# First attention: modulation products in half chunks on two column groups, sent by SyncE, and the bias of two-tile units added by TensorE

## The chip, the cores and the metric

The kernel runs as one program on one core of a Trainium2 chip. The metric is the device time in microseconds (us), as the median of several executions. A core has TensorE (PE: matmuls, with a weight load of its own ahead of each), VectorE (DVE), ScalarE (ACT), GpSimd (POOL) and SyncE (SP). Here SP only sends transfers. Each engine works off its own instructions in order, and they wait for each other by semaphores.

## The reference, cut to what matters

Two models in a row: a block of two layers (a differential attention with a bias by position, a latent attention, each with a gated FFN and a per-layer embedding), and a second block of two layers whose normed input is scaled and shifted by modulation vectors. All numbers are float32. The change touches the differential attention of the first layer and the modulation of the second block's first layer:

```
sc = einsum('bqhcd,bkhcd->bhcqk', q_blk, k) * scale          # 8 heads, c = 2
sc = where(causal_mask(i, s), sc + bias, NEG_INF)            # bias[h, q, k]
a = softmax(sc, axis=-1)
wts = a[:, :, 0] - lam * a[:, :, 1]
o = einsum('bhqk,bkhv->bqhv', wts, v)
o = rms_norm(o, sub_gain) * (1.0 - lam_init)                 # then @ w_o
...
mod_x = (silu_c @ w_mod[i] + b_mod[i])                       # 1024 -> 3072
mod_c = silu_cc @ w_mod[i] + b_mod[i]
sh_x, sc_x, g_x = split(mod_x, 3)
hx = rms_norm_2(x, norm_g[i]) * (1.0 + sc_x) + sh_x
```

There are 256 tokens, 1024 features, 8 heads of this attention. The modulation vectors depend on `c` and `c_ctx` alone, so they can be computed at any time before the second block.

## The kernel before, in words

Weights stream through the kernel in 295 panels of 512 KB. SP sends each into one of six raw slots (L380), in the order of use; it sends panel p when the low half of panel p - 5 has been split off. ACT makes the high half WH (L1817), DVE the low half WL (L1123), and PE multiplies three times (L413 to L415).

The first attention stands between the projections (`first_unit`) and the output projection `l0_o` (`gemm_unit`, panels 24 to 31). It has 16 units: 8 heads by 2 query tiles. A unit of query tile 0 sees one key tile (128 keys), a unit of query tile 1 sees two (256 keys). The order of the work is written out by hand, as a loop over n in which each engine takes another unit. In round n PE does the two score products of unit n (L724), then five modulation products (`fill(filler)`, L559), the values of a head whose two units are done (L732, written to G), and the transposes of the probabilities of unit n - 2 (`turn`, L633). DVE adds the bias to the scores of unit n (L1351), takes the row maximum (L1204), and scales the probabilities of unit n - 1 (L1179 to L1185). ACT does the exponentials (L1867) and copies the transposed probabilities (L1856) and the values (L1966). POOL squares each head's result (L2479).

After the last unit come the norms of heads 0 to 3 and 4 to 7: the sum over squares on DVE (L1356), the root on ACT (L1976), the reciprocal (L1363) and the products (L1367) on DVE, the transposes on PE (`heads_turn`, L741), and the two halves of the result: XH by ACT (L1982), XL by DVE (L1376). The first unit of `l0_o` starts with heads 0 to 3. On ACT the order is: transposed heads 0 to 3 (L1982), then the root of heads 4 to 7 (L1976).

The modulation vectors of the second block come from products with a stationary tile of 32 columns (`SC[:, k, :]`, silu of `c` and `c_ctx`, the other columns zero) and moving tiles of `w_mod`. The output is 32 partitions of the bank O. The first 2048 of the 3072 columns are made in this attention, as 16 blocks of 128 columns; each block needs 8 products (k = 0 to 7), 128 products in all. They stand as fillers: 12 before the attention, 5 in each of 18 rounds, then 14, 6 and 6 around the transposes of the heads. Block i goes to partitions 32 * (i // 4) and up, so that four blocks in a row go to the same 32 partitions (one column group of TensorE's array). POOL sends the blocks, 512 KB each, into six slots (RN, L2453): two after the first and two after the second step of the bias, the others after `bias_ok`, each when its slot has been used. The remaining 1024 columns and the second layer's come in the FFNs, as `modulate` (L547): four products of 512 columns to four column groups in a row.

Of the kernel before, what the change touches and what calls it, by code (L numbers as in the profile page):

```python
# [32 lines left out]
SPL = 3  # L33
# [3 lines left out]
RMS = 6  # L37
PLAIN = 16
CHUNKS = 8
# [10 lines left out]
START = {}  # L50
# [55 lines left out]
TBLOCKS, TVALS = _b, _v  # L106
# [29 lines left out]
def program(nc, x_tok, wst, wmod, vec, cst, x_t, ctx_t, p_t, pos, pos4, tab, rpb, lam4, grow, y_t):  # L136
    with ExitStack() as ctx:
# [3 lines left out]
        def sem(name):  # L141
            return ctx.enter_context(nc.semaphore(name))
# [25 lines left out]
        SC = sb("SC", [P, KD, 32])  # L168
# [11 lines left out]
        KT0 = mv[:, 2048:4096].rearrange("p (n t) -> p n t", t=T)  # L180
# [14 lines left out]
        TB = B[:, 0:3072].rearrange("p (h k) -> p h k", h=8)  # L195
# [25 lines left out]
        RN = mv[:, 6144:12288].rearrange("p (s c) -> p s c", s=RMS)  # L221
# [61 lines left out]
        def bc(ap, n):  # L283
            return ap.unsqueeze(1).broadcast_to([P, n, ap.shape[1]])
# [38 lines left out]
        m_zero, m_sil, m_used, m_y, m_tr, m_ok = (sem("m_zero"), sem("m_sil"), sem("m_used"), sem("m_y"), sem("m_tr"),  # L323
                                                  sem("m_ok"))
        m_raw = [sem(f"m_raw{i}") for i in range(RMS)]
        sum_step = sem("sum_step")
        r_raw = [sem(f"r_raw{i}") for i in range(2)]
        r_vec = [sem(f"r_vec{i}") for i in range(2)]
# [44 lines left out]
        @block.sync  # L373
        def _(sp):
            sp.dma_start(V[:, :], vec).then_inc(in_vec, 16)

            def panel(p, slot, freed):
                if freed is not None:
                    sp.wait_ge(w_lo, freed)
                sp.dma_start(RAW[:, slot, :], w_ap[p]).then_inc(w_raw[slot], 16)  # L380

            for s in range(RAWS):
                panel(s, s, None)
                if s == 0:
                    sp.dma_start(H[:, 0:4, :], x_t[:, 0:4, :]).then_inc(in_x, 16)
                    sp.dma_start(H[:, 4:8, :], x_t[:, 4:8, :]).then_inc(in_x2, 16)
                if s == 2:
                    sp.dma_start(XTOK, x_tok).then_inc(in_xt, 16)
                if s == 3:
                    sp.dma_start(C[:, :], cst).then_inc(in_cst, 16)  # L390
            turns = NPAN // RAWS
            with sp.Fori(1, turns) as i:
                for s in range(RAWS):
                    panel(i * RAWS + s, s, i * RAWS + s - RAWS + 1)
            for p in range(turns * RAWS, NPAN):
# [9 lines left out]
        def _(pe):  # L405
# [144 lines left out]
            def fill(n):  # L550

                for _ in range(n):
                    i, k = divmod(fills[0], KD)
                    if fills[0] == 0:
                        pe.wait_ge(m_sil, 1)
                    if k == 0:
                        pe.wait_ge(m_raw[i % RMS], 16 * (i // RMS + 1))
                    g, q = i // 4, i % 4
                    m = mm(O[32 * g:32 * g + 32, q * P:(q + 1) * P], SC[:, k, :], RN[:, i % RMS, k * P:(k + 1) * P],  # L559
                           start=(k == 0), stop=(k == KD - 1), skip_group_check=True)  # L560
                    if k == KD - 1:
                        m.then_inc(m_used, 1)
                    fills[0] += 1

            def turn_modulators(dst, made):
# [38 lines left out]
                for _ in range(n):  # L604
                    next(unit, None)

            def attention(s, scores, value, filler=0, behind=None, meanwhile=(0, 0), first=0, last=None, ready=()):
                units = attn_units(s)
                width = 1 if s == "l0" else 2
                for n in range(first, len(units) + 3 if last is None else last):  # L610
                    if behind is not None and n > len(units):
                        advance(behind, meanwhile[n - len(units) - 1])
                    if n < len(units):
                        a = AU0[s] + n
                        if a >= 2:
                            pe.wait_ge(at_ex, 2 * (a - 1))
                        scores(A[2 * (a % 2):2 * (a % 2) + 2], units[n]).then_inc(at_s, 1)
                    if n < len(units) + 2:
                        fill(filler)
                    def turn():  # L620

                        if 2 <= n <= len(units) + 1:
                            nk = units[n - 2][2]
                            a = AU0[s] + n - 2
                            for u, copied in ready:
                                if n - 2 == u:
                                    pe.wait_ge(tm_v, copied)
                            pe.wait_ge(at_p, a + 1)
                            if a >= 1:
                                pe.wait_ge(at_tc, a)  # L630
                            for c in range(width):
                                for k in range(nk):
                                    m = nc.tensor.transpose(ST[c][:, k * P:(k + 1) * P],  # L633
                                                            PRB[a % 3][:, c, k * P:(k + 1) * P], IDT)
                            m.then_inc(at_t, 1)

                    def values():

                        if n >= 3 and units[n - 3][4]:
                            p, qt, nk, job, last = units[n - 3]  # L640
                            pe.wait_ge(at_tc, AU0[s] + n - 2)
                            j = AJ0[s] + job
                            if j >= 2:
# [77 lines left out]
            def scores_l0(out, unit):  # L721
                h, qt, nk, *_ = unit
                for c in range(2):
                    m = mm(out[c][:, 0:nk * P], QT[64 * c:64 * c + 64, h, qt * P:(qt + 1) * P],  # L724
                           KT0[64 * c:64 * c + 64, h, 0:nk * P], start=True, stop=True, skip_group_check=True)
                return m

            def value_l0(out, pt, unit):
# [15 lines left out]

            pe.wait_ge(tm_ev, 8)
            pe.wait_ge(tm_v, 4)
            fill(12)
            pe.wait_ge(bias_ok, 1)
            attention("l0", scores_l0, value_l0, 5)
            fill(14)  # L750
            heads_turn(0)
            fill(6)
            heads_turn(1)
            fill(6)
            for u in range(4):
                gemm_unit(U0["l0_o"] + u, START["l0_o"] + 2 * u, 0, KD, 8, 2,
                          fresh=[XS["l0_o"] - 4] * 4 + [XS["l0_o"]] * 4 if u == 0 else None)
# [114 lines left out]
            for u, (name, g, kt, panels) in enumerate(TOKEN):  # L872
# [22 lines left out]
                if 4 <= u <= 8:  # L895
                    for r in range(2 * u - 8, min(2 * u - 6, 9)):
# [5 lines left out]
            attention("l1", scores_l1, value_l1, 0, first_o, (4, 3), first=2, ready=((1, TVALS),))  # L902
            advance(first_o, 32)
            pe.wait_ge(at_g, AJ0["a"])
            for u in range(1, 4):
# [112 lines left out]
            attention("a", scores_a, value_a, 0, first_o, (2, 2), first=4)  # L1018
            advance(first_o, KD)
            for u in gemm_wide("a_o", 5, None, 1):  # L1020
                pass
# [70 lines left out]
            attention("b", scores_b, value_b, 0, first_o, (6, 3), first=2, ready=((0, TVALS + 10), (1, TVALS + 12)))  # L1092
# [17 lines left out]
        def _(dv):  # L1110
# [236 lines left out]

            def bias_l0(sc, un):
                h, qt, nk, *_ = un
                k0 = 0 if qt == 0 else P  # L1350
                return v.tensor_tensor(sc, sc, bc(TB[:, h, k0:k0 + nk * P], 2), ALU.add)  # L1351

            def heads_summed(g):

# [981 lines left out]
        def _(gp):  # L2336
# [111 lines left out]
            def panels(first, end):  # L2448

                for i in range(first, end):  # L2450
                    if i >= RMS:
                        gp.wait_ge(m_used, i - RMS + 1)
                    gp.dma_start(RN[:, i % RMS, :], wmod[i // 2].rearrange("p (h c) -> (p h) c", h=2)[P * (i % 2):P * (i % 2) + P, :]).then_inc(m_raw[i % RMS], 16)  # L2453

            def gathers(layer, k, i):

# [24 lines left out]
            nextp = 4  # L2481
            for h in range(8):
                upto = min(PLAIN, 6 + (10 * h + 35) // 8)
                panels(nextp, upto)
                nextp = upto
                head_squares(h)
            sum_of_squares("ffn0", H, after("l0_o"))
            ffn(0)
# [203 lines left out]
```

## Time and profile before

| | |
|---|---|
| runs | 1317.41 us median of 3 (1317.01 to 1320.32) |
| the profiled execution | its own time 1318.33 us, span 1316.6 us |
| granted clock of TensorE, mean | 0.997 of full speed |
| busy | PE 1259.6, PE's weight loads 1089.8, DVE 883.2, ACT 689.6, POOL 364.9 us |
| modulation products of the first attention (L559) | 256 records for 128 products, 31.4 us busy, 96.0 to 149.3 us |
| score products (L724) | 64 records for 32 products |
| transfers of `w_mod` by POOL | 16 of 512 KB (this stage), 16 of 1 MB (the FFNs) |

The span is what the profiler saw; the execution's own time has about 1.7 us around it. A float32 product is two records in the trace, so "x10" is five products. Records of PE are longer than the step to the next one, since matmuls overlap; the chain of waits and the starts in a timeline show the step. DVE, ACT and POOL have one record per instruction. In a row of windows the last three numbers are the granted clock of TensorE (1.00 is 2.4 GHz, 0.50 is 1.2 GHz), the busy share of the DMA engines and GB/s; ahead of them stand the stretch, its length and each engine's busy time.

### The profile page before, as it was taken

Reading aid. Unit: us, or ns where it says so; the run is one execution under the profiler, and the core shown is the slowest. Engines: PE = TensorE matmul, PEld = TensorE weight load, DVE = VectorE, ACT = ScalarE, POOL = GpSimd, SP = SyncE. Lnnn points to the kernel's source line nnn. Section 1 sums busy time; section 2 is a strip of 40 time slices with the busy share of each in tenths; the row PEclk is TensorE's granted clock in tenths of the full one; section 3 lists DMA queues with packets and bytes.
Section 4 is the critical chain, followed back from the end, with each engine's and each line's share of the span. In section 5 each row is a group of like instructions: output and inputs, shape, how many; then the busy total and the mean of one; then the engine's idle time right before and its main releaser. Section 6 shows DMA issues by size and latency. Waiting matters only on the chain.

```text
span 1316.6 us, 24170 instructions
## 1 busy us (share of the span) xinstructions
PE 1259.6 (96%) x8884; PEld 1089.8 (83%) x8884; DVE 883.2 (67%) x1388; ACT 689.6 (52%) x1217; POOL 364.9 (28%) x377
## 2 busy tenths in 40 slices
PE   6999999999999999999999999999989999999996
PEld 4887899999998877898999998888755699987666
DVE  6878588666768985558976667753377548453674
ACT  5555455444567777545554447544367515413562
POOL 4942145344321140144444332011012220000022
PEclk9999999999999999999999999999999999999998
DMA  8565247566545532255665664422200364522100
GB/s 311 178 219 193 65 144 263 202 237 237 198 144 175 165 124 96 67 190 173 228 227 208 236 206 135 134 73 95 95 1 1 71 170 144 160 97 80 49 1 33
DMA packets 50361, 191.72 MB, mean 146 GB/s; under 512 B 5792, under 2 KB 6048, under 8 KB 47968
## 3 DMA queue, kind: packets, MB, share of 16 engines
q1 hardware_dynamic: 43488, 158.59, 36.5%
q0 software_dynamic: 6064, 31.33, 6.8%
q8 instruction: 62, 1.02, 0.3%
q10 hardware_dynamic: 720, 0.57, 0.2%
q14 instruction: 27, 0.22, 0.1%
HBM read 189.41 MB, written 1.05 MB: 145 GB/s over the span
## 4 chain that ended last, share of the span: by engine, by line
PE 78%; DVE 9%; ACT 7%; issue 3%; DMA 1%; POOL 1%; SPq 0%; DVEq 0%; ACTq 0%; POOLq 0%
PE G L413 14%; PE G L415 13%; PE G L414 13%; PE A L413 6%; PE A L415 6%; PE A L414 6%; DVE WL L1123 3%; PE R L633 3%; PE R L559 2%; ACT WH L1817 2%; PE A L991 1%; PE R L413 1%; PE R L415 1%; PE R L414 1%; PE G L1000 1%
## 5 line engine op out<-in xcount | busy, mean ns | idle before, releaser
L1123 DVE TENSOR_TENSOR WL<-RAW,WH 128x1024 fp32r<-128x1024 f32 x295 | 382.2, 1302 | 291.8 <-ACT WH L1817 291.4
L1817 ACT ACTIVATE WH<-RAW 128x1024 fp32r<-128x1024 f32 x295 | 310.4, 1057 | 415.1 <-PE G L415 302.7
L413 PE MATMUL G<-XH,WH 128*128 128x256 f32 (+1 forms) x1336 | 400.1, 299 | 9.6 <-DVE WL L1123 6.3
L414 PE MATMUL G<-XL,WH 128*128 128x256 f32 (+1 forms) x1336 | 394.9, 296 | 0.0
L415 PE MATMUL G<-XH,WL 128*128 128x256 f32 (+1 forms) x1336 | 394.9, 296 | 0.0
L413 PEld LDWEIGHTS G<-XH,WH 128*128 128x128 f32 x1336 | 255.3, 191 | 33.2 <-issue 25.8
L414 PEld LDWEIGHTS G<-XL,WH 128*128 128x128 f32 x1336 | 255.5, 191 | 6.3
L415 PEld LDWEIGHTS G<-XH,WL 128*128 128x128 f32 x1336 | 255.5, 191 | 6.3
L413 PE MATMUL A<-HH,WH 128*128 128x256 f32 x352 | 99.8, 283 | 3.7 <-POOL HL L2432 3.7
L414 PE MATMUL A<-HL,WH 128*128 128x256 f32 x352 | 99.6, 283 | 0.0
L415 PE MATMUL A<-HH,WL 128*128 128x256 f32 x352 | 99.5, 283 | 0.0
L2408 POOL CAST XH<-HRS 128x256 fp32r<-128x256 f32 x24 | 11.4, 474 | 267.3 <-DVE HRS L1714 267.3
L1204 DVE TENSOR_REDUCE SM<-A 128x2 f32<-128x1024 f32 (+1 forms) x80 | 67.8, 849 | 17.9 <-PE A L991 12.9
L413 PEld LDWEIGHTS A<-HH,WH 128*128 128x128 f32 x352 | 67.6, 192 | 4.1 <-ACT WH L1817 4.1
L2428 POOL TENSOR_TENSOR HRS<-HSQ,HRS 128x256 f32<-128x256 f32 x22 | 32.0, 1456 | 128.6 <-ACT HRS L2027 128.6
L415 PEld LDWEIGHTS A<-HH,WL 128*128 128x128 f32 x352 | 67.6, 192 | 0.0
L414 PEld LDWEIGHTS A<-HL,WH 128*128 128x128 f32 x352 | 67.6, 192 | 0.0
L1856 ACT ACTIVATE ATT<-R 128x1024 f32<-128x1024 f32 (+3 forms) x56 | 37.7, 674 | 56.9 <-PE R L633 56.9
L413 PE MATMUL G<-WH,XH 128*128 128x512 f32 (+1 forms) x136 | 54.8, 403 | 12.5 <-DVE XL L1149 11.1
L2428 POOL TENSOR_TENSOR HRS<-ATT,HRS 128x256 f32<-128x256 f32 x22 | 32.1, 1457 | 98.1 <-ACT HRS L2027 92.6
L413 PE MATMUL A<-WH,XH 128*128 128x512 f32 x144 | 57.3, 398 | 1.5 <-DVE XL L1444 1.3
L415 PE MATMUL A<-WH,XL 128*128 128x512 f32 x144 | 56.2, 390 | 0.0
(345 smaller groups left out, 2364.7 us busy)
## 6 DMA issues: line engine op xcount, KB each, us to landing
RAW<-in_wst SPq DMA_DIRECT2D x295, 512.0 KB, 3.8
M<-in_wmod POOLq DMA_DIRECT2D x16, 1024.0 KB, 6.6
M<-in_wmod POOLq DMA_DIRECT2D x16, 512.0 KB, 6.3
B<-in_rpb POOLq DMA_DIRECT2D x4, 1024.0 KB, 12.0
H<-in_x_t SPq DMA_DIRECT2D x2, 512.0 KB, 8.3
M<-in_x_tok SPq DMA_DIRECT2D x1, 1024.0 KB, 13.4
M<-in_ctx_t POOLq DMA_DIRECT2D x1, 1024.0 KB, 5.1
out_y<-M SPq DMA_DIRECT2D x2, 384.0 KB, 2.7
```

Source lines behind the costliest of these rows:

```text
L413: mm(out, lh, rh, start=start, stop=False, skip_group_check=True)
L414: mm(out, lh, rl, start=False, stop=False, skip_group_check=True)
L415: return mm(out, ll, rh, start=False, stop=stop, skip_group_check=True)
L559: m = mm(O[32 * g:32 * g + 32, q * P:(q + 1) * P], SC[:, k, :], RN[:, i % RMS, k * P:(k + 1) * P], start=(k == 0), stop=(k == KD - 1), ski ...
L633: m = nc.tensor.transpose(ST[c][:, k * P:(k + 1) * P], PRB[a % 3][:, c, k * P:(k + 1) * P], IDT)
L991: m = mm(out[c][:, 0:nk * P], Q2[64 * c:64 * c + 64, t, qt * P:(qt + 1) * P], K2[64 * c:64 * c + 64, t // 4, k0:512], start=True, stop=Tru ...
L1000: m = mm(out[64 * c:64 * c + 64, 0:T], V2[:, k + (0 if nk == 4 else 2), kv * 64:(kv + 1) * 64], pt[:, c, k, :], start=(k == 0), stop=(k == ...
L1123: v.tensor_tensor(WL[:, slot, :], RAW[:, raw, :], WH[:, slot, :].bitcast(F32), ALU.subtract).then_inc(w_lo, 1)
L1204: v.tensor_reduce(small(80, a, 2), sc, AX, ALU.max, negate=True).then_inc(at_mx, 1)
L1817: act(WH[:, slot, :], RAW[:, raw, :], ACT.Copy).then_inc(w_hi, 1)
L1856: act(att(s, j)[:, 0:width, 0:nk, q * P:(q + 1) * P], RO[:, :].rearrange("p (l k q) -> p l k q", l=2, k=4)[:, 0:width, 0:nk, :], ACT.Copy) ...
L2428: g.tensor_tensor(HID[b], CB[b][:, 0, :], SG[b], ALU.mult).then_inc(f_hid, 1)
```

## The change

1. `w_mod` is laid out otherwise. A chunk is now one k (128 rows) by 1024 of the first 2048 columns. There are still 16 chunks of 512 KB; chunk i has k = i // 2 and half i % 2.
2. `fill` takes a whole chunk: two products of 512 columns with the same stationary tile, to the two column groups 2 * half and 2 * half + 1. There are 32 products instead of 128.
3. They stand in another order: two chunks before the attention, one in each of rounds 1 to 14, none in rounds 0 and 15 to 17, and none around the transposes of the heads.
4. POOL sends chunks 0 to 5 only, the last two after `bias_ok`. SP sends chunks 6 to 15 between panels 32 and 33, each after a wait on the count of used chunks; its loop over panels is cut in two for that.
5. For a unit with two key tiles the bias is added by PE: behind the two score products come two products of the identity with the bias, 256 columns each, into the same banks. DVE adds it only for units with one key tile.

```
-                    i, k = divmod(fills[0], KD)
-                    if k == 0:
-                        pe.wait_ge(m_raw[i % RMS], 16 * (i // RMS + 1))
-                    g, q = i // 4, i % 4
-                    m = mm(O[32 * g:32 * g + 32, q * P:(q + 1) * P], SC[:, k, :], RN[:, i % RMS, k * P:(k + 1) * P],
-                           start=(k == 0), stop=(k == KD - 1), skip_group_check=True)
+                    i = fills[0]
+                    k, half = divmod(i, 2)
+                    pe.wait_ge(m_raw[i] if i < RMS else m_next[i % RMS], 16 * max(1, i // RMS))
+                    for g in range(2):
+                        r = 32 * (2 * half + g)
+                        m = mm(O[r:r + 32, :], SC[:, k, :], RN[:, i % RMS, 512 * g:512 * g + 512],
+                               start=(k == 0), stop=(k == CHUNKS - 1), skip_group_check=True)
+                    m.then_inc(m_used, 1)
...
-                    if n < len(units) + 2:
-                        fill(filler)
+                    if n in filler:
+                        fill(1)
...
                     m = mm(out[c][:, 0:nk * P], QT[64 * c:64 * c + 64, h, qt * P:(qt + 1) * P],
-                           KT0[64 * c:64 * c + 64, h, 0:nk * P], start=True, stop=True, skip_group_check=True)
+                           KT0[64 * c:64 * c + 64, h, 0:nk * P], start=True, stop=qt == 0, skip_group_check=True)
+                if qt:
+                    for c in range(2):
+                        m = mm(out[c][:, 0:nk * P], IDT, TB[:, h, P:P + nk * P], start=False, stop=True, skip_group_check=True)
...
-            fill(12)
+            fill(2)
             pe.wait_ge(bias_ok, 1)
-            attention("l0", scores_l0, value_l0, 5)
-            fill(14)
+            attention("l0", scores_l0, value_l0, range(1, 15))
             heads_turn(0)
-            fill(6)
             heads_turn(1)
-            fill(6)
...
+            held = START["l0_o"] + SPL + RAWS
+            for i in range(RMS, PLAIN):
+                sp.wait_ge(m_used, i - RMS + 1)
+                sp.dma_start(RN[:, i % RMS, :], wmod[i // 2][:, PW * (i % 2):PW * (i % 2) + PW]).then_inc(m_next[i % RMS], 16)
...
-                k0 = 0 if qt == 0 else P
-                return v.tensor_tensor(sc, sc, bc(TB[:, h, k0:k0 + nk * P], 2), ALU.add)
+                return None if qt else v.tensor_tensor(sc, sc, bc(TB[:, h, 0:P], 2), ALU.add)
```

What stands on PE in rounds 3 and 4 of the attention. Before: L724 are the scores, L559 the modulation products, L633 the transposes, L732 the values.

```order
L724 MATMUL A<-M 128x256 x2
L559 MATMUL R<-M,SC 32x128 x5
L633 MATMUL R<-C,RSQ 128x128 x2
L724 MATMUL A<-M 128x128 x2
L559 MATMUL R<-M,SC 32x128 x5
L732 MATMUL G<-M,ATT 128x128 x3
L633 MATMUL R<-C,HSQ 128x128
```

After (L739 scores, L743 bias, L575 modulation, L648 transposes, L750 values):

```order
L739 MATMUL A<-M 128x256 x2
L743 MATMUL A<-B,C 128x256 x2
L575 MATMUL R<-M,SC 32x512 x2
L648 MATMUL R<-C,RSQ 128x128 x2
L739 MATMUL A<-M 128x128 x2
L575 MATMUL R<-M,SC 32x512 x2
L750 MATMUL G<-M,ATT 128x128 x3
L648 MATMUL R<-C,HSQ 128x128
```

Two bias products have come in behind the scores with two tiles, and each five products of 128 columns are two of 512.

The end of the attention on PE, from the last scores to the output projection. Before (L741 are the transposes of the heads, L413 the projection):

```order
L559 MATMUL R<-M,SC 32x128 x5
L633 MATMUL R<-C,ATP 128x128 x2
L732 MATMUL G<-M,ATT 128x128 x3
L559 MATMUL R<-M,SC 32x128 x14
L741 MATMUL A<-C,B 128x128 x8
L559 MATMUL R<-M,SC 32x128 x6
L741 MATMUL A<-C,B 128x128 x8
L559 MATMUL R<-M,SC 32x128 x6
L413 MATMUL G<-XH,WH 128x256
```

After (L759 are the transposes of the heads):

```order
L739 MATMUL A<-M 128x256 x2
L743 MATMUL A<-B,C 128x256 x2
L648 MATMUL R<-C,RSQ 128x128 x2
L750 MATMUL G<-M,ATT 128x128 x3
L648 MATMUL R<-C,HSQ 128x128
L648 MATMUL R<-C,ATP 128x128 x2
L750 MATMUL G<-M,ATT 128x128 x3
L759 MATMUL A<-C,B 128x128 x16
```

No modulation product stands behind the last scores any more, and the transposes of the heads follow each other.

SP's queue around the modulation chunks, after (L381 are panels, L405 chunks of `w_mod`):

```order
L381 DMA RAW<-in_wst 128x1024 x3
L405 DMA M<-in_wmod 128x1024 x10
L381 DMA RAW<-in_wst 128x1024 x3
```

The ten chunks stand between panels 30 to 32 and 33 to 35. In before POOL had them, between its squares of the heads.

## Rows read from the trace of the kernel before

**Rows 1.** The page, busy time of each engine.

```profile
PE 1259.6 (96%) x8884; PEld 1089.8 (83%) x8884; DVE 883.2 (67%) x1388; ACT 689.6 (52%) x1217; POOL 364.9 (28%) x377
```

**Rows 2.** Chain of waits in the attention: start us, us on the chain, what.

```profile
98.82 0.44 PE A L724 x4
...
106.04 0.37 PE R L633 x2
...
106.83 1.21 PE R L559 x10
108.04 0.86 PE G L732 x6
108.91 0.11 PE R L633
109.02 0.63 PE A L724 x4
...
121.28 0.79 PE R L559 x10
```

**Rows 3.** Chain of waits at the attention's end.

```profile
133.35 0.71 DVE A L1351
...
138.51 0.45 PE R L633 x2
...
139.42 0.94 PE G L732 x6
140.36 3.17 PE R L559 x28
...
149.37 0.32 PE G L413
```

**Rows 4.** Timelines of DVE and ACT there: start us, us, what [idle before].

```profile
141.99 1.22 DVE L1356 TENSOR_REDUCE SM<-HRS 128x8 f32<-128x1024 f32 x1 [0.50 <-POOL HRS L2479]
...
147.15 2.72 DVE L1376 SCALAR_TENSOR_TENSOR XL<-A,SM,XH 128x512 fp32r<-128x512 f32 x4
...
144.22 1.26 ACT L1982 ACTIVATE XH<-A,SM 128x512 fp32r<-128x512 f32 x2 [3.44 <-PE A L741]
145.37 0.30 ACT L1976 ACTIVATE SM<-SM 128x8 f32<-128x8 f32 x1
```

**Rows 5.** PE's timeline in the first FFN, four column groups.

```profile
231.55 0.28 PE L415 MATMUL A<-HH,WL 128*128 128x256 f32 x1
231.75 1.06 PE L547 MATMUL R<-M,SV 128*32 128x512 f32 x8
232.75 0.38 PE L413 MATMUL G<-XH,WH 128*128 128x256 f32 x1
```

**Rows 6.** PE's timeline in the second attention, two full-array products, then their successor.

```profile
518.80 1.03 PE L854 MATMUL A<-M 128*128 128x256 f32 x4
519.76 0.70 PE L857 MATMUL A<-B,M 64*128 64x256 f32 x4
```

**Rows 7.** DMA issues from 98 to 99.4 us: KB each, us to landing.

```profile
M<-in_wmod POOLq DMA_DIRECT2D x1, 512.0 KB, 6.1
```

**Rows 8.** PE's timeline at the start, the longest gap of the body, the end; clock of a stretch.

```profile
11.10 0.77 PE L413 MATMUL G<-WH,XH 128*128 128x512 f32 x1 [11.10 <-DVE XL L1149]
...
15.08 0.63 PE L413 MATMUL G<-WH,XH 128*128 128x512 f32 x1
15.51 0.47 PE L414 MATMUL G<-WL,XH 128*128 128x512 f32 x1
...
16.05 0.39 PE L413 MATMUL G<-WH,XH 128*128 128x512 f32 x1
...
375.60 0.36 PE L413 MATMUL A<-HH,WH 128*128 128x256 f32 x1 [1.86 <-POOL HL L2432]
...
1307.04 0.70 PE L468 MATMUL R<-ATP,C 128*128 128x256 f32 x2 [0.59 <-ACT ATP L2327]
...
1309.00:1309.50 0.50, 0.00 (x0) 0.00 (x0) 0.50 (x1) 0.00 (x0) 0.00 (x0) 0.81 0.00 0
```

More of the change, by code:

```diff
@@ L325, in program @@
         m_raw = [sem(f"m_raw{i}") for i in range(RMS)]
+        m_next = [sem(f"m_next{i}") for i in range(RMS)]
         sum_step = sem("sum_step")
@@ L391, in _, with trip @@
             turns = NPAN // RAWS
-            with sp.Fori(1, turns) as i:
+            held = START["l0_o"] + SPL + RAWS
+            def trip(i):
                 for s in range(RAWS):
                     panel(i * RAWS + s, s, i * RAWS + s - RAWS + 1)
+            with sp.Fori(1, held // RAWS) as i:
+                trip(i)
+            for p in range(held // RAWS * RAWS, held):
+                panel(p, p % RAWS, p - RAWS + 1)
+            for i in range(RMS, PLAIN):
+                sp.wait_ge(m_used, i - RMS + 1)
+                sp.dma_start(RN[:, i % RMS, :], wmod[i // 2][:, PW * (i % 2):PW * (i % 2) + PW]).then_inc(m_next[i % RMS], 16)
+            for p in range(held, (held // RAWS + 1) * RAWS):
+                panel(p, p % RAWS, p - RAWS + 1)
+            with sp.Fori(held // RAWS + 1, turns) as i:
+                trip(i)
             for p in range(turns * RAWS, NPAN):
@@ L552, in fill @@
                 for _ in range(n):
-                    i, k = divmod(fills[0], KD)
-                    if fills[0] == 0:
+                    i = fills[0]
+                    k, half = divmod(i, 2)
+                    if i == 0:
                         pe.wait_ge(m_sil, 1)
-                    if k == 0:
-                        pe.wait_ge(m_raw[i % RMS], 16 * (i // RMS + 1))
-                    g, q = i // 4, i % 4
-                    m = mm(O[32 * g:32 * g + 32, q * P:(q + 1) * P], SC[:, k, :], RN[:, i % RMS, k * P:(k + 1) * P],
-                           start=(k == 0), stop=(k == KD - 1), skip_group_check=True)
-                    if k == KD - 1:
-                        m.then_inc(m_used, 1)
+                    pe.wait_ge(m_raw[i] if i < RMS else m_next[i % RMS], 16 * max(1, i // RMS))
[4 more added lines that the diff above has]
+                    m.then_inc(m_used, 1)
                     fills[0] += 1
@@ L605, in advance, with attention @@
                     next(unit, None)
-            def attention(s, scores, value, filler=0, behind=None, meanwhile=(0, 0), first=0, last=None, ready=()):
+            def attention(s, scores, value, filler=(), behind=None, meanwhile=(0, 0), first=0, last=None, ready=()):
                 units = attn_units(s)
@@ L901, in _ @@
                                 + [(1, k) for k in range(8, 16)], T, lambda k: pe.wait_ge(at_g, AJ0["l1"] + k // 2 + 1))
-            attention("l1", scores_l1, value_l1, 0, first_o, (4, 3), first=2, ready=((1, TVALS),))
+            attention("l1", scores_l1, value_l1, (), first_o, (4, 3), first=2, ready=((1, TVALS),))
             advance(first_o, 32)
@@ L1017, in _ @@
             evacuated(pe, U0["a_z"] + 7)
-            attention("a", scores_a, value_a, 0, first_o, (2, 2), first=4)
+            attention("a", scores_a, value_a, (), first_o, (2, 2), first=4)
             advance(first_o, KD)
@@ L1091, in _ @@
             first_o = head_unit("b_o", [(c, k) for c in range(2) for k in range(7)] + [(0, 7), (1, 7)], T, lambda k: pe.wait_ge(at_o, AT_JOBS["a"] + k + 1))
-            attention("b", scores_b, value_b, 0, first_o, (6, 3), first=2, ready=((0, TVALS + 10), (1, TVALS + 12)))
+            attention("b", scores_b, value_b, (), first_o, (6, 3), first=2, ready=((0, TVALS + 10), (1, TVALS + 12)))
             advance(first_o, 2 * KD)
@@ L2452, in panels @@
                         gp.wait_ge(m_used, i - RMS + 1)
-                    gp.dma_start(RN[:, i % RMS, :], wmod[i // 2].rearrange("p (h c) -> (p h) c", h=2)[P * (i % 2):P * (i % 2) + P, :]).then_inc(m_raw[i % RMS], 16)
+                    gp.dma_start(RN[:, i % RMS, :], wmod[i // 2][:, PW * (i % 2):PW * (i % 2) + PW]).then_inc(m_raw[i % RMS], 16)
             def gathers(layer, k, i):
@@ L2479, in head_squares @@
                 g.tensor_tensor(HRS[:, :, (h % 4) * P:(h % 4 + 1) * P], o, o, ALU.mult).then_inc(hn_sq, 1)
-            nextp = 4
+            panels(4, RMS)
             for h in range(8):
-                upto = min(PLAIN, 6 + (10 * h + 35) // 8)
-                panels(nextp, upto)
-                nextp = upto
                 head_squares(h)
@@ L2641 @@
     wmod = np.concatenate([a["w_mod_2"][i] for i in range(2)], 1)
-    near = _tiles(wmod[:, :PLAIN * P]).reshape(PLAIN, PT, P, P).transpose(0, 2, 1, 3).reshape(CHUNKS, P, 2 * PW)
-    far = wmod[:, PLAIN * P:].reshape(KD, P, 2, 2 * PW).transpose(2, 0, 1, 3).reshape(2 * CHUNKS, P, 2 * PW)
-    wmod = np.ascontiguousarray(np.concatenate([near, far]))
+    wmod = np.ascontiguousarray(wmod.reshape(KD, P, 3, 2 * PW).transpose(2, 0, 1, 3)).reshape(3 * KD, P, 2 * PW)
     def twice(x):
```

## The prediction

> **What bounds the kernel now.** I read the page first: TensorE (PE) is busy 96% of the span [rows 1], so a change is worth what it takes from PE's line, or from a wait that PE stands in. Then the chain of waits from 95 to 150 us. The reader is to see that from the first scores at 98.82 us until 133.35 us every piece of the chain is PE's: scores, modulation products (L559), transposes (L633), values (L732), one after the other with no gap [rows 2]. From 133.35 us on VectorE (DVE) and ScalarE (ACT) stand in it [rows 3]. So the stage has two parts with different limits: 34.5 us of PE work end to end, then a tail of latencies. Last I read the timelines of DVE and ACT in the tail for what each step there needs [rows 4].
>
> A check of the first part: up to the last scores, 8 pairs of scores (0.42, the first 0.44, and 0.63), 15 slots of five products (1.21 each, one of them 0.79), turns of 0.37 and 0.11 (one of 0.26), six values of 0.86 [rows 2] make 8.4 + 17.7 + 3.1 + 5.2 = 34.4 us, against 34.5 from 98.82 to 133.35. The model holds, so I replace terms in it.
>
> **The change, part by part.** The sum is made in the profiled execution: span 1316.6 us, its own time 1318.33; the median of the runs is 1317.41, 0.9 lower, and differences are carried over to it.
>
> 1. Modulation products. Gone: 128 products of 128 columns, 0.242 us each (1.21 / 5). New: 16 chunks, each two products of 512 columns for two column groups, F us a chunk. F is not in the trace of before. What is: four such products for four column groups, which take 0.99 us to the next matmul and 1.08 us with the gap before them [rows 5]. Serially, four times 4 x 0.242 would be 3.9, so groups overlap. A second sign: the slot in which the group changes takes 0.79 instead of 1.21 [rows 2]. Below, one product of 512 columns can't take less than four of 128 without their fixed part, about 0.88. So F is 0.88 to 1.08; I take 0.97. Fourteen chunks come before the last scores: 14 x 0.97 = 13.6 instead of 17.7.
>
> The first two chunks go ahead of the attention (0.99 [rows 5] instead of 12 x 0.242), but the attention can't begin before DVE has made the bias, just ahead of the first scores at 98.82 [rows 2]; so that is worth nothing.
>
> 2. Bias of the two-tile units. TensorE adds it with two 128x256 products per unit, B us a unit, 8 units, all on PE's line. Two such full-array products take 0.96 us to their successor in the second attention [rows 6]; without a fixed part twice 0.43. So B is 0.87 to 0.96; I take 0.92: 8 x 0.92 = 7.4 us more. DVE loses eight additions of 0.71, but in the first part DVE isn't on the chain, so only the last is worth something: it stands on the chain at 133.35 us [rows 3].
>
> First part: 13.6 + 7.4 - 17.7 = 3.3 us later at the last scores. With the DVE addition gone: 2.6 us later at the end of the last value (140.36 in before).
>
> 3. The tail. Between the last value and the first matmul of the output projection before has 3.17 us of products (14 of them) [rows 3] and twice six more. All of them go, and the head transposes come as soon as DVE is ready. What is late next is the norm of heads 4 to 7. Its sum (L1356) ends at 143.15 us, 2.8 after the last value, and that doesn't change. In before its square root (L1976) waits until 145.37, because ACT stands in L1982, which waits for transposes that stand behind the 14 products [rows 4]. Now those transposes end at about 1.8 after the value and ACT is free at 2.5. So: root 3.1, reciprocal 3.4, two products of DVE to 4.7, two of the four L1376 (2.72 / 4 each) to 6.1, projection at 6.2 after the value. Before: 149.37 - 140.36 = 9.0. The tail gives 2.8 us.
>
> Sum so far: +2.6 - 2.8 = -0.2 us; with the bounds of F and B from -2.1 to +1.6.
>
> 4. Sending. Ten chunks move from POOL's queue to SP's. There they stand behind panel 32 and ahead of panel 33, whose slot comes free only when the projection (149.37 us [rows 3]) has used a panel; so no weight waits for them. SP waits on the counts of used chunks there, the last (chunk 9) in the middle of the attention. But SP sends chunks 6 and 7 as soon as panel 32 is out and chunks 0 and 1 are used, beside chunks 4 and 5, which POOL still sends at about 99 after the bias. Chunk 4 took 6.1 us to land in before [rows 7], at 105.1; it is needed after the scores of rounds 0 to 3, one turn of 0.26 and chunks 2 and 3, at 98.8 + 2.4 + 2 B + 2 F = 105.0. A wait of 0 to 2.2 us (a third more to land, with two chunks more in the air); I take 0.3, since its issue is the same and only its neighbours change. Moving it off POOL frees 0.5 us a chunk there, which nobody on the chain waits for.
>
> 5. The clock. Cover is gone in the tail: PE's last piece before DVE is done ends 1.9 us after the last scores (turn, value, turn), and the last two transposes of the attention come 4.5 after them (138.51 - 133.29 - 0.71 [rows 3]): empty for 2.6 us. Between the head transposes it is empty from 1.8 to 4.1 us after the value, 2.3 us, and around these gaps stand mostly transposes. In the body of before the longest empty stretch is 1.86 us, with dense work around it, and the clock stays at the full 2.4 GHz [rows 8]. At the end of the kernel the granted clock falls to 1.2 GHz at about 1309.3 us, 1.6 us after the last of a few sparse products [rows 8]. The new tail looks more like the latter. What half speed costs: the first matmuls of the kernel, from 11.10 to 15.5 us, last 0.63 us and start 0.43 apart, the same matmuls from 16.05 on last 0.39 [rows 8], so 4.4 us at the lower level (though the clock's column names it full there), half of it lost: 2.2 us if it all falls on the projection. Bounds: 0 (the clock stays) and 3.5 (the last value and transposes too). I take 2.2.
> The Trainium skill speaks against the change here too: TensorE: Matmul & The Clock Gate (Part 4: PE-mode transpose) says that a transpose doesn't count as a busy TensorE for the clock. By that the tail would be nearly empty from the last scores on; if transposes did count, the fall would be less likely. No row of before settles it.
>
> Total: -0.2 + 0.3 + 2.2 = +2.3 us, 1317.41 + 2.3 = 1319.7.
>
> **The rivals.**
> The clock stays. For it: 1.86 us empty cost nothing twice [rows 8]. Against: the gaps are longer and lie close together. Then the sum is +0.1: 1317.5.
>
> Two groups don't overlap (slower). Place: the 14 slots between scores. If the second product began only with the second half of the first, F would be three halves of 0.43 to 0.45 plus 0.1, or 1.4; wholly serial 1.77 to 1.85. Price: 14 x 0.43 = 6 us to 14 x 0.85 = 12 us: 1325 to 1331. It decides from F = 1.25. For it: scores of 256 columns, two products on two row groups, take 0.63 and not the 0.44 of one [rows 2]. Against: four groups in 0.99 us [rows 5].
> By the Trainium skill (TensorE: Matmul & The Clock Gate, Part 3: Packing small matmuls) matmuls start strictly in program order, and an fp32 product is two records here, so the 1.4 would follow; the same page has three column groups at 2.38 times the speed. The row with four groups fits the second.
>
> Chunks come late (also slower). SP's two early chunks halve what POOL's 4 and 5 get, chunk 4 lands at 107 or later, and chunk 5 too: 2 to 5 us more, 1320 to 1324. Against: SP's land before POOL's first byte, if before's rate there holds.
>
> The products hide beside other matmuls (faster). They use 64 of 128 columns. If the slots of 0.97 shrank by half, 7 us: 1310 to 1312. Against: in before no piece beside a slot got shorter except where the column group changed [rows 2]. That the change doesn't do what it says would show as F = 4 x 0.242 twice, which is the serial case.
>
> **How the numbers follow.** Clock falls: 0.47, 1319.7 (own range 1317.5 to 1321.6). Clock stays: 0.36, 1317.5 (1315.3 to 1319.4). No overlap 0.07; late chunks 0.05; hidden products 0.05. The bound of what can be told from no change is 0.3%, or 4 us: 1313.4 to 1321.4. Faster: the last case, 0.05. Slower: no overlap, half of the late chunks, and the upper end of the falling clock (0.07), 0.17. Same: 0.78. The range goes from the lower end of the staying clock to just above the upper end of the falling clock, 1315.2 to 1321.9; it leaves out the two ends and the rare cases.
>
> **What would show it.** The slots of the modulation products after the scores: 0.97 us each (1.4 or more: no overlap). Bias products: 0.92 us behind each two-tile score. Last scores at about 136.6 us, last value ending at 143, first matmul of the projection at about 149.5. A wait of PE for chunk 4 near 105 us. The granted clock between 138 and 155 us: matmuls of the projection 0.21 us apart at first instead of 0.12 means it fell. From the second unit of the projection on, all must be as before, shifted. The prediction is wrong if the projection starts before 147 or after 152 us, or if the total moves while that start doesn't.

## The result and the profile after

| | before | changed |
|---|---|---|
| time, median of 5 | 1319.06 us (1317.01 to 1320.32) | 1326.05 us (1323.99 to 1329.91) |
| ratio | | 1.0058 (95%: 1.0045 to 1.0071) |
| profiled execution, span | 1316.6 us | 1324.9 us |
| mean granted clock | 0.997 | 0.990 |

The change makes the kernel 7.0 us slower. Forecast were 1319.7 us and a range to 1321.9, from a base of 1317.41 us; the five runs of before here have their median at 1319.06, so 1.65 us of the miss are the base, and the other 4.7 are the difference between +7.0 and the forecast +2.3. Three executions of the case took 1590, 1759 and 3155 us and stay out of all ratios. The page of the changed kernel has TensorE as busy as before [rows 1], over a longer span:

```profile
PE 1260.9 (95%) x8724; PEld 1078.0 (81%) x8724; DVE 876.8 (66%) x1380; ACT 690.0 (52%) x1217; POOL 360.5 (27%) x367
```

Where did the time go? I set the same gaps of TensorE in both traces beside each other. The gap before the first FFN's input is at 178.79 us in before and at 185.44 in the changed kernel, 6.65 later. But the first scores start at 97.35 us instead of 98.77 (both from TensorE's timeline), mostly by chance: the first matmul starts at 9.92 instead of 11.10 [rows 8], and over the eleven variants below that start varies from 9.90 to 11.36. So between the first scores and that gap 8.1 us are lost. Until 382 us nothing more is. There is one more piece, 1.5 us, in a part of the program that the change doesn't touch (below).

The chain of waits in the attention of the changed kernel (start us, us on the chain, what), against [rows 2]:

```profile
98.11 9.90 DMA M<-in_wmod
108.05 1.92 PE R L575 x4
109.97 1.58 PE G L750 x6
...
111.77 1.16 PE A L739 x4
112.92 1.46 PE A L743 x4
114.39 0.98 PE R L575 x4
...
117.14 0.87 PE G L750 x6
118.11 0.63 PE A L739 x4
118.75 1.06 PE A L743 x4
```

There are three things to see. The chain runs over a transfer of `w_mod` issued at 98.11 us: chunk 5. Behind it the same instructions take nearly twice as long (values 1.58 and then 0.87, scores 1.16 and then 0.63, the modulation chunk 1.92 and then 0.98). And in the undisturbed rounds a chunk costs 0.98 us, as forecast, but the bias pair L743 costs 1.06, more than my upper bound of 0.96.

TensorE's timeline in the same kernel (start us, us, what, idle before it and its releaser) shows the waits and the tail:

```profile
97.35 0.93 PE L739 MATMUL A<-M 64*128 64x128 f32 x8 [1.66 <-DVE SM L1361]
...
105.51 1.05 PE L575 MATMUL R<-M,SC 128*32 128x512 f32 x4 [1.83 <-DMA M<-in_wmod]
...
108.05 1.92 PE L575 MATMUL R<-M,SC 128*32 128x512 f32 x4 [0.40 <-DMA M<-in_wmod]
...
140.37 1.13 PE L743 MATMUL A<-B,C 128*128 128x256 f32 x4
141.33 0.38 PE L648 MATMUL R<-C,RSQ 128*128 128x128 f32 x2
...
145.91 0.44 PE L648 MATMUL R<-C,ATP 128*128 128x128 f32 x2 [2.46 <-DVE ATP L1200]
...
152.29 1.97 PE L759 MATMUL A<-C,B 128*128 128x128 f32 x8 [1.99 <-DVE B L1381]
154.30 0.55 PE L428 MATMUL G<-XH,WH 128*128 128x256 f32 x1
154.65 0.42 PE L429 MATMUL G<-XL,WH 128*128 128x256 f32 x1
154.87 0.42 PE L430 MATMUL G<-XH,WL 128*128 128x256 f32 x1
...
158.20 0.28 PE L428 MATMUL G<-XH,WH 128*128 128x256 f32 x1
158.32 0.28 PE L429 MATMUL G<-XL,WH 128*128 128x256 f32 x1
```

Chunk 4 is waited for 1.83 us, chunk 5 another 0.40. In the tail the two gaps of 2.46 and 1.99 us are there. The projection starts at 154.30 with its matmuls 0.22 us apart, and only from 158.20 on they are 0.12 apart. That slow start costs 1.65 us: from the projection's first matmul to the gap at 178.79 and 185.44 it is 29.49 us in before and 31.14 here. The last bias pair (140.37) takes 0.96 us to the transposes behind it, not 1.06; that is taken up again in the section on the prediction. Windows of the same kernel (stretch, its length, TensorE busy, granted clock, DMA share, GB/s) show the clock at these times:

```profile
104.00:106.00 2.00, 0.49 (x4) 1.00 1.02 399
106.00:108.00 2.00, 1.66 (x10) 0.72 1.06 412
110.00:112.00 2.00, 2.00 (x9) 0.50 0.51 145
114.00:116.00 2.00, 2.00 (x12) 1.00 0.00 0
146.00:148.00 2.00, 1.28 (x8) 0.96 0.00 0
148.00:150.00 2.00, 1.67 (x8) 0.50 0.00 0
156.00:158.00 2.00, 2.00 (x11) 0.50 0.04 8
158.00:160.00 2.00, 2.00 (x19) 0.98 0.00 0
```

TensorE was busy for 0.49 of the 2 us from 104 to 106, and then the clock fell to 1.2 GHz, from about 107 to 113.7 us. It fell a second time at 148, until 158. The DMA engines are fully busy at the first fall and idle at the second. The issues from 98 to 99.4 us, which answer to [rows 7]:

```profile
M<-in_wmod POOLq DMA_DIRECT2D x2, 512.0 KB, 8.9
M<-in_wmod SPq DMA_DIRECT2D x1, 512.0 KB, 9.7
```

The 8.9 us are the median of two. Narrower windows of the same view separate them: chunk 4 takes 7.9 us to land (6.1 in before) and chunk 5 9.9. They also show what is in flight beside them. SP issues chunk 6 at 97.1 us, ahead of POOL's chunk 4 (97.6), and it lands in 5.5 us; chunk 7 follows at once and takes 9.7; chunks 8 and 9 go out at 100.3 and 101.8 us, when chunks 2 and 3 have been used. In before chunks 6 and 7 were issued from 100.3 us on, behind 4 and 5 in POOL's queue, and chunks 8 and 9 at 103.6 and 106.3.

The last piece of the time stands at a gap that before has as well [rows 8]:

```profile
382.25 0.36 PE L428 MATMUL A<-HH,WH 128*128 128x256 f32 x1 [1.86 <-POOL HL L2446]
```

and the window behind it, in the columns of the windows above:

```profile
384.00:385.00 1.00, 1.00 (x7) 0.50 0.64 160
```

The same 1.86 us, and this time the clock falls behind it. The next gap (399.46 in before, 407.56 here) is 8.10 us later instead of 6.65, so this fall costs 1.45 us. All 13 profiles of this case have this gap, 1.84 to 1.86 us long; behind it the clock fell in five of them (the changed kernel, e2, e4, e9, e12) and stayed at 1.00 in the other eight, before among them. Nothing here ties it to the change.

### The profile page after: what moved, and what is told of

Read it like the earlier page. It is cut to its first block, busy times and chain, and to the rows that moved or that the text cites. A ratio compares the mean times of both kernels' runs of the same rounds, so it can differ in the third digit from the quotient of the medians.

```text
span 1324.9 us, 23824 instructions
## 1 busy us (share of the span) xinstructions
PE 1260.9 (95%) x8724; PEld 1078.0 (81%) x8724; DVE 876.8 (66%) x1380; ACT 690.0 (52%) x1217; POOL 360.5 (27%) x367
## 4 chain that ended last, share of the span: by engine, by line
PE 79%; DVE 8%; ACT 7%; issue 3%; DMA 1%; POOL 1%; DVEq 0%; SPq 0%; ACTq 0%; POOLq 0%
PE G L428 14%; PE G L429 13%; PE G L430 13%; PE A L428 6%; PE A L430 6%; PE A L429 6%; DVE WL L1138 3%; PE R L648 3%; ACT WH L1831 2%; PE R L428 1%; PE R L430 1%; PE R L429 1%; PE A L1006 1%; PE G L1015 1%; PE R L562 1%
## 5 line engine op out<-in xcount | busy, mean ns | idle before, releaser
L429 PE MATMUL A<-HL,WH 128*128 128x256 f32 x352 | 100.3, 285 | 0.0
```

The lines of the kernel that those rows point to most:

```text
L429: mm(out, lh, rl, start=False, stop=False, skip_group_check=True)
```

## The experiments

All times are medians in us, beside runs of the kernel before on the same chip (1319.15 us beside e1 to e4, 1318.57 beside e5 and e9 to e11, 1318.23 beside e12 to e14). "Stage" is the time from the first scores to the first matmul of the projection in the profiled execution. It is 50.5 us in before and 57.0 in the changed kernel, which then loses 1.65 us more on the projection's slow start.

| run | what | stage | total | ratio to before, 95% |
|---|---|---|---|---|
| e1 | SP sends chunks 4 and 5 first | 51.9 | 1323.78 | 1.0041 (1.0027 to 1.0055) |
| e2 | products of zeros in the waits | 55.0 | 1324.86 | 1.0046 (1.0032 to 1.0059) |
| e3 | products of zeros in the tail | 54.2 | 1323.85 | 1.0034 (1.0024 to 1.0043) |
| e4 | bias by DVE | 50.3 | 1321.03 | 1.0015 (1.0005 to 1.0024) |
| e5 | POOL sends all | 53.2 | 1322.57 | 1.0030 (1.0019 to 1.0040) |
| e9 | e1 and e4 | 48.1 | 1316.55 | 0.9985 (0.9976 to 0.9994) |
| e10 | e9 with zeros around | 47.7 | 1313.96 | 0.9965 (0.9953 to 0.9976) |
| e11 | e9, chunks moved to the tail | 43.1 | 1311.10 | 0.9947 (0.9934 to 0.9960) |
| e12 | before, bias by TensorE alone | 58.6 | 1327.36 | 1.0070 (1.0057 to 1.0083) |
| e13 | e11 with bias by TensorE | 47.7 | 1316.13 | 0.9986 (0.9978 to 0.9995) |
| e14 | e11 with five more zeros | 42.7 | 1311.90 | 0.9958 (0.9944 to 0.9971) |

Single executions of a variant lie 1.5 to 7 us apart, those of before about 3. So terms of 1 to 3 us are read from the traces, and the medians only confirm their sum.

**e1: who comes first on the DMA engines.**

```
+            sp.wait_ge(bias_ok, 1)
+            for i in range(4, RMS):
+                sp.dma_start(RN[:, i % RMS, :], wmod[i // 2][...]).then_inc(m_raw[i], 16)
             for i in range(RMS, PLAIN):      # SP
...
-            panels(4, RMS)                   # POOL
```

> The changed kernel, but SP sends chunks 4 and 5 too, ahead of 6 to 15, after a wait on the bias; POOL sends none of the last twelve. Theory (chunks 4 and 5 land late because SP's 6 to 9 take their share of the DMA engines from another queue): chunk 4 lands in 4 to 6 us, PE waits 0 to 0.3 us for it instead of 2.2, the clock stays at 1.00 in the attention, first scores to first projection matmul 52.0 us instead of 57.0, total about 4.9 us below the changed kernel (1321). Rival (all transfers together are too many, whoever sends them): the wait stays near 2 us, total 1326.

Its stage is 51.9 us, 5.0 less than in the changed kernel. TensorE's timeline has the products of chunks 4 and 5 with no wait:

```profile
104.59 1.13 PE L746 MATMUL A<-B,C 128*128 128x256 f32 x4
105.65 1.05 PE L578 MATMUL R<-M,SC 128*32 128x512 f32 x4
...
107.42 1.05 PE L578 MATMUL R<-M,SC 128*32 128x512 f32 x4
```

and its windows show the granted clock at 1.00 from 98 to 138 us, though the DMA engines are as full as before:

```profile
98.00:106.00 8.00, 6.61 (x35) 1.00 0.88 277
106.00:114.00 8.00, 8.00 (x44) 1.00 0.98 384
```

So it isn't the amount of transfers but their order that costs the wait. The run changes the queue of chunks 4 and 5 together with their place; e5, with all chunks in POOL's queue, has no wait either. Which of SP's chunks 6 to 9 took most of the share no run separates. The profiled span is 5.2 us below the changed kernel's, the median only 2.3. In this profile the clock fell at 22.9 us too, at a gap of 2.77 us in the first projection (1.60 us in the changed kernel's profile, with the clock at 1.00), and the attention began 2 us later. The fall in the tail is still there.

**e2: is the slow stretch the clock's?**

```
+                    if i in (4, 5):
+                        idle(8 if i == 4 else 2)
                     pe.wait_ge(m_raw[i] ...)
+            def idle(n):
+                for _ in range(n):
+                    mm(O[0:30, 0:P], SC[:, 0, 2:32], IDT, start=False, stop=True, skip_group_check=True)
```

> The changed kernel with ten products of zeros (128 columns, added to O) in the two waits for chunks 4 and 5. Theory (the wait of 2.2 us costs 2.7 us more because the clock falls after it): the waits stay, the clock stays at 1.00 from 98 to 140 us, stage 57.0 - 2.7 = 54.3 us, total 1323.3. Rival (the slow stretch at 108 to 114 us has another cause, such as the DMA traffic): still slow, total 1326.

The stage is 55.0 us, 2.0 less, and the clock stays at 1.00 from 104 to 144 us. But in this execution it fell earlier: from about 97 to 100.7 us it was at 0.50, after the gap of 1.67 us before the first scores. That makes TensorE ask later: it is ready for chunk 4 at 105.19 us, and the chunk, issued at 97.7, lands 8.5 us later, at 106.2. So about 1.0 us of waiting is left in place of 1.83, and the zeros cover it, until 106.74. The run agrees with the theory and doesn't isolate it, since the wait shrank as well. What it adds is that the gap that the change opens ahead of the attention (12 products became two chunks) can cost as well; I had put that edit at nothing.

**e3: the tail.**

```
+                    if s == "l0" and n == 17:
+                        idle(9)
                     def turn():
...
+            idle(1)
             heads_turn(0)
+            idle(7)
             heads_turn(1)
```

> The changed kernel with products of zeros in the gaps behind the last scores: nine in the last round before the transposes, one before and seven between the transposes of the heads. Theory (the clock falls in the tail because PE is empty): the clock stays at 1.00 to the projection, whose matmuls start 0.12 us apart at once; 1.9 us less there and about 1.0 less on transposes, total 1323.2. Rival (transposes alone let the clock fall, or the fillers delay the transposes): first projection matmuls still 0.21 us apart, total 1326 or above.

The projection starts at full pace, 0.12 us between its second and third product in TensorE's timeline:

```profile
151.83 0.35 PE L428 MATMUL G<-XH,WH 128*128 128x256 f32 x1 [0.76 <-DVE XL L1399]
152.03 0.28 PE L429 MATMUL G<-XL,WH 128*128 128x256 f32 x1
152.15 0.28 PE L430 MATMUL G<-XH,WL 128*128 128x256 f32 x1
```

and the windows of this run have full clock in the whole tail:

```profile
97.00:104.00 7.00, 6.39 (x22) 0.51 0.87 269
...
144.00:154.00 10.00, 7.80 (x58) 1.00 0.01 2
```

From the start of the last value to the projection it takes 7.15 us instead of 7.48, and the 1.65 us of slow start are gone: 2.0 us for the clock of the tail, close to the 2.2 of the forecast. The fall ahead of the attention came here too (0.51 from 97 to 104 us).

**e4: the bias back on DVE.**

```
-                if qt:
-                    for c in range(2):
-                        m = mm(out[c][:, 0:nk * P], IDT, TB[:, h, P:P + nk * P], ...)
+                return v.tensor_tensor(sc, sc, bc(TB[:, h, k0:k0 + nk * P], 2), ALU.add)
```

> The changed kernel with the bias of all units added by DVE again, as in before; the rest stays. Theory (TensorE's bias costs 8 x 1.06 us on its line and gives back 0.7): pairs of rounds take 4.4 us instead of 5.42, unless DVE is the bound, at 4.1 to 4.5; five free pairs and the first two: 6 us less, but chunk 4 is asked for 2 us earlier and waited for longer, so about 1322. Rival (DVE would have been the bound without TensorE's help): pairs of 5 us or more, total 1325 to 1327.

Stage 50.3 us, 6.7 less. The timeline of TensorE, one wait and one pair of rounds:

```profile
107.55 1.28 PE L575 MATMUL R<-M,SC 128*32 128x512 f32 x4 [4.03 <-DMA M<-in_wmod]
...
117.18 0.70 PE L739 MATMUL A<-M 64*128 64x256 f32 x4
117.81 1.05 PE L575 MATMUL R<-M,SC 128*32 128x512 f32 x4
...
121.54 0.70 PE L739 MATMUL A<-M 64*128 64x256 f32 x4
```

A pair is 121.54 - 117.18 = 4.36 us against 5.42 in the changed kernel and 4.81 in before, with no gap: DVE keeps up, and the rival falls. Part of the gain is eaten by the chunk, asked for sooner and waited for 4.03 us.

**e5: POOL sends all chunks again.** SP's ten sends are gone; POOL sends up to chunk 9 before its first head and two more per head.

> The changed kernel, but POOL sends all chunks in order, as in before (up to chunk 9 before its first head, two more per head). Only the sender is undone. Theory (chunks 6 to 9 in SP's queue take the share of 4 and 5): POOL's own queue keeps the order, chunk 4 lands as in before or sooner (6 us or less), wait for it 0 to 0.8 us instead of 1.83 and 0.40; the clock in the attention stays; stage 52 to 53 us, total 1321 to 1322. Rival (a software queue mixes its own chunks as much): wait about 2 us, total 1326.

There is no wait for a chunk, and chunk 4 lands in 6.6 us. The ratio to before is 1.0030 instead of 1.0058. But the clock was at 0.50 from 100 to 103 us in this execution, so that TensorE asked later. At full clock it would ask 6.3 us after the first scores, at 105.0, and the chunk landed at about 105.5: a wait of half a us, by this estimate. No run shows it.

**e9: both costs out.** e1 and e4 together.

> The changed kernel with two parts altered: SP sends chunks 4 and 5 first, and DVE adds all biases. Theory (late chunks and the bias on TensorE are the two costs beside the clock): no wait for chunks, pairs of 4.36 us as in the run with the bias on DVE, last scores about 30.3 us after the first, then 7.0 + 7.5 us; stage about 45.5 us against 50.5 in before, less 2 us of clock in the tail: total 1319.1 - 5 + 2 = 1316. Rival (chunks are asked for sooner, and even SP's order is too late): a wait of 1 to 2 us and the clock falls in the attention, total 1319 to 1320.

The total, 1316.55 us, is the first below that of before. The stage, 48.1 us, is longer than the theory had it, since a wait is left:

```profile
104.55 1.05 PE L578 MATMUL R<-M,SC 128*32 128x512 f32 x4 [1.80 <-DMA M<-in_wmod]
```

The rival was right about the wait and the clock (0.50 around 107 us), and wrong about the total.

**e10: the clock kept.** e9 with the zeros of e3 and six more ahead of the attention.

> As the run before this one (SP sends chunks 4 and 5, DVE adds the bias), and products of zeros: six ahead of the attention, nine before the last transposes, one and seven at the transposes of the heads. Theory (an empty TensorE lowers the clock before and behind the attention): clock 1.00 from 94 us to the projection, 2 to 3 us less than without them: 1313.5, and runs closer together. Rival (the fillers cost as much as they keep): the same time as without, 1316.

2.6 us below e9, with intervals that just touch. The fall in the tail, which e9's profile has, is gone (1.00 from 110 to 146 us); ahead of the attention neither profile has one. The fall behind the wait for chunk 4 (2.05 us) stays. The fillers keep more than they cost.

**e11: real work in the gaps.**

```
-            attention("l0", scores_l0, value_l0, range(1, 15))
+            attention("l0", scores_l0, value_l0, (1, 2, 4, 5, 7, 8, 10, 11, 13, 14))
...
+                    if s == "l0" and n == 17:
+                        fill(2)
...
             heads_turn(0)
+            fill(2)
             heads_turn(1)
```

> SP sends chunks 4 and 5, DVE adds the bias, six products of zeros ahead of the attention; of the 14 chunks in the rounds four are moved into the gaps of the tail (two before the last transposes, two between the transposes of the heads), so that real products keep TensorE busy there; rounds 3, 6, 9 and 12 have none. Theory: four times 0.98 us go from TensorE's line into gaps, but DVE then paces the rounds at 4.1 to 4.2 us a pair instead of 4.36; 1 us below the run with zeros, 1312.5. Rival (DVE or the softmax chain paces at 4.4 or more): the same as with zeros, 1313.5.

1311.10 us, 7.5 below before and 2.9 below e10; I had expected 1 of these. Chunk 4 is asked for a round later and waited for 0.16 us only. That part I hadn't counted. DVE is now on the chain in the rounds. The tail, TensorE's timeline:

```profile
129.92 1.07 PE L578 MATMUL R<-M,SC 128*32 128x512 f32 x8
132.45 0.44 PE L658 MATMUL R<-C,ATP 128*128 128x128 f32 x2 [1.46 <-DVE ATP L1209]
...
134.87 1.97 PE L766 MATMUL A<-C,B 128*128 128x128 f32 x8 [0.49 <-DVE B L1391]
136.77 1.94 PE L578 MATMUL R<-M,SC 128*32 128x512 f32 x8
```

Two chunks of different halves take 1.07 us together at full clock (129.92), and 1.94 where the clock has fallen (136.77): four column groups at once. So in a place for two chunks the second costs nearly nothing. The clock fell at about 134 us in this profile, behind a gap of 1.46 us that ends at 132.45.

**e12: the bias alone, on the kernel before.**

> The kernel before with one part of the change alone: TensorE adds the bias of the two-tile units. Theory (1.06 us a unit on TensorE's line, 0.7 once back from DVE): pairs of rounds take 5.87 us instead of 4.81, stage 50.5 + 8 x 1.06 - 0.7 = 58.3 us, no clock loss since the fillers stay; total 1318.6 + 7.8 = 1326.4. Rival (the products overlap with the modulation products, or DVE paced before): 2 to 4 us, total 1321 to 1323.

8.1 us more in the stage, 9.1 in the total (0.7% slower, a little more than expected). The profile has the fall behind the gap of 1.86 us, which before's has not. The chain of waits there:

```profile
115.44 0.86 PE G L735 x6
...
116.42 0.63 PE A L724 x4
117.05 1.06 PE A L728 x4
```

L728 is the bias pair, 1.06 us, all of it on the chain. This one part alone costs more than the whole change, which gets some of it back from the modulation products and the tail.

**e13: the bias on TensorE in the best arrangement.**

> The run with work in the tail, but with the bias of the two-tile units on TensorE: the change as it is, with chunks 4 and 5 sent first, four chunks in the tail, and six products of zeros ahead of the attention. Theory: TensorE paces the rounds again (3.26 + 0.14 + 2/3 of 1.96 = 4.7 us a pair, against 4.0 to 4.2 with DVE's bias), 4 us more than there: 1315. Rival (DVE paces there, and relieving it is worth what TensorE loses): 1311.

1316.13 us, 5.0 above e11, and the stage 4.6 longer. Where DVE paces the rounds at 4.0 us a pair, relieving it is still worth less than 1.06 us of TensorE.

**e14: e11 and five zeros before the last transposes.**

> The run with work in the tail plus five products of zeros before the last two transposes of the attention, where 1.46 us stayed empty. Theory (that gap lets the clock fall at 134.5 us): the clock stays to the projection, 1.5 us less on the transposes of the heads and the projection's start: 1309.6. Rival (the fall comes from the transposes, or varies by run): 1311.

The clock stays at 1.00 from 94 us to the projection in its profile, and the stage is 0.3 us shorter. The median is 1311.90 us, and its interval overlaps with e11's: no difference shown.

## Why the prediction was wrong

The step that failed is step 4, the sending. I gave the wait for chunk 4 0 to 2.2 us and took 0.3, "since its issue is the same and only its neighbours change". It was 2.23 us (1.83 for chunk 4, 0.40 more for chunk 5), the upper end. TensorE asked when I had said, 6.3 us after the first scores (forecast 6.2); what came late was the chunk, 7.9 us in flight instead of 6.1. I had counted SP's chunks 6 and 7 as neighbours and had them land first. Chunk 6 went out ahead of chunk 4, chunk 7 was still in flight when chunk 4 landed, and SP sent 8 and 9 from its own queue 2 and 3 us sooner, counted from the first scores, than POOL did in before. e1 puts 4 and 5 ahead of all of these and has no wait.

With it failed the price of a wait. I had put the clock into the tail only. The wait empties TensorE, and the clock falls behind it. All four profiles with a wait of 1.80 us or more for chunk 4 (the changed kernel, e4, e9, e10) have a granted clock of 0.50 within 3 us of its end; in all the others it is at 1.00 from 104 us to the tail. In the chain the pieces behind chunk 5 take 0.94 + 0.71 + 0.10 + 0.53 + 0.40 = 2.7 us more than the same pieces later on, and the scores just before chunk 5 0.80 instead of 0.49 (TensorE's timeline). The late-chunk rival had this mechanism, without the clock: a chance of 0.05 and a price of 2 to 5 us.

Step 2 was mis-sized: B is 1.06 us in seven of the eight units, outside 0.87 to 0.96, which makes 1.0 us in all. In the eighth unit it is 0.96. What differs is the product behind the pair: where a modulation product of 32 columns follows, the step is 1.06, and where a transpose follows it is 0.96 or 0.97. e13 has both, 1.06 in the five units with a chunk behind the pair and 0.97 in the three without one. The row that I took B from [rows 6] has no product of 32 columns behind it.

The rest held. F is 0.98 us against 0.97: the column groups overlap, and the rival of program order falls. The last value starts 5.3 us after the end of the last bias, the projection 6.5 us after the last value (forecast 6.2). The clock falls in the tail and costs 2.0 us (forecast 2.2), by e3. The first chunks were put at nothing. The gap of 1.66 us that they leave ahead of the attention had the clock fall behind it in three of the seven profiles without fillers there (e2, e3, e5).

The sum: forecast +2.3, wait +1.9, slow scores +0.3, clock behind the wait +2.7, B +1.0, clock of the tail -0.2, makes +8.0 us, against 8.1 in the trace. The forecast's range ended at 1321.9 because it took the bounds of the wait without what hangs on its upper one. One of the recorded signs of being wrong came: the projection starts at 154.30 us, after 152. Two slips of the working change nothing: with the lower bounds of F and B the sum is -1.9 us, not -2.1, and the sum over squares ends at 143.21 us [rows 4], not 143.15.

From the sentence of the Trainium skill (TensorE: Matmul & The Clock Gate, Part 3: Packing small matmuls) that matmuls start in program order I had worked out 1.4 us for a chunk; the same section's speedups spoke for less, and the measured 0.98 is on their side. Its Part 4 (PE-mode transpose) says that a transpose doesn't count as a busy TensorE in the same way. No run here decides on that, since in the tail the empty gaps were filled and the transposes stayed.

## What to carry to other kernels

When transfers are moved to another queue, write down which of them are in flight together and which is needed first. The two queues shared the DMA engines here: chunk 4 took 7.9 us with four of SP's chunks around it, and 5.7 (e1) or 6.6 (e5) with all chunks in one queue in the order of use. Price every wait of TensorE twice, once as the wait and once as the clock that may fall behind it; waits of 2.2 us cost 2.7 us more here, and the two gaps of the tail 2.0. Fillers on TensorE in a tail of latencies look free to remove, but they keep the clock up, so taking them out gives back less than it seems. Real work moved there was the best variant (0.9947 of before).

## What was not expected of the hardware

The clock's fall doesn't follow from the length of a gap alone. Behind the same gap of 1.86 us it fell in five profiles of 13, and behind the gap of 1.66 us ahead of the attention in three of seven. The falls that could be priced cost 1.45, 2.0 and 2.7 us. The executions of the changed kernel go with it: the slowest, 1329.91 us, has a mean granted clock of 0.986, the two fastest 0.992 and 0.993. That this is why they spread over 6 us, and those of before over 3, is likely and not shown.

Products of zeros on 30 columns ran beside the modulation products in e2 at little cost. Two of them with chunk 5 took 1.07 us to the next instruction, against 0.98 for a chunk alone, while eight of them with nothing beside took about 1.6 us.
